# A two-layer hybrid encoder: high and low x as one moving operand for the high gate/up weights, and the filter network moved

## The chip, the cores and the metric

One core of a Trainium2 chip. The metric is the device time of one execution in microseconds, the median of several runs. The profile is one execution of the same program, taken by the hardware profiler.

## The reference

Two layers over x of 256 x 1024, all in float32. A layer is a half-weighted gated feed-forward block, a mixer of three parts, and a second feed-forward block with its own weights.

```python
def swiglu_ffn(x, w_gate, w_up, w_down):
    return (jax.nn.silu(x @ w_gate) * (x @ w_up)) @ w_down

def hyena_filters(L, w1, b1, f1, w2, b2, f2, w3):
...
    h = jnp.sin(f1 * (z @ w1 + b1))
    h = jnp.sin(f2 * (h @ w2 + b2))
    h = (h @ w3).astype(jnp.float32).reshape(L, HY_ORDER, 2, HY_WIDTH)
...
def hybrid_layer(x, ...):
    x = x + 0.5 * swiglu_ffn(rms_norm(x, ffn1_norm), ffn1_w_gate, ffn1_w_up, ffn1_w_down)
    proj = rms_norm(x, mix_norm) @ w_in
...
    x = x + jnp.concatenate([y_hy, y_mla, y_gla], axis=-1) @ w_out
    x = x + 0.5 * swiglu_ffn(rms_norm(x, ffn2_norm), ffn2_w_gate, ffn2_w_up, ffn2_w_down)
    return x
```

The gate and up weights are 1024 x 2816, the down weights 2816 x 1024. The filter network (`hyena_filters`) does not depend on x: z is a constant table of 256 positions by 33, and its hidden width is 64.

## The kernel before

**Split products.** The matmuls run on a rounded float32 form (`F32R`). To keep precision, each operand is split: a high part (the rounded copy) and a low part (what is left of it). A product is three matmuls: high by high, high by low, low by high. `passes` (L1034 to L1038) issues the three: L1036 high weights with high x, L1037 high weights with low x, L1038 low weights with high x. The profile's `xT_high`, `xT_low` are XH and XL, the transposed x of 8 tiles (k) of 128 x 256.

**Weights.** All weights come as a stream of slots of 128 x 2048 (1 MB), fetched by SP into three buffers (`raw`). ScalarE makes the high part of a slot (`hi`, L409), VectorE the low part (`lo`, L681); each has three buffers, too, so that slot n can be converted once slot n - 3 has been used by TensorE. A feed-forward stage has 33 slots: for each of 11 chunks of 256 hidden columns, two gate/up slots (one for each half of 128 hidden columns, gate and up weights of all 8 k) and one down slot.

**A feed-forward stage** (four in all: two in each layer, `f` = 0 and 1). TensorE transposes x (`turn_x`, L1065); ScalarE and VectorE write XH and XL (L425, L691) from the transposes, two tiles a group. Then TensorE runs the two gate/up slots of chunk 0, a row of reciprocal norms (`rstd_row`, L1072), and for every later chunk c: gate/up half 0 of chunk c, half 1 of chunk c, down of chunk c - 1. A gate/up slot (`gate_up`) is 2 x 8 triples of 256 moving columns: for gate (g = 0) and up (g = 1), over the 8 k, accumulated in one half each of a PSUM bank. Banks 4 to 7 hold two chunks' halves (`4 + 2 * pr + half`, where `pr` alternates), banks 0 to 3 the down product. A down slot is 8 triples of 512 columns.

**Each half of a chunk** goes through a chain: VectorE multiplies the gate with the norms' row (`gate_normed`, L706), ScalarE takes the silu (L457), VectorE multiplies with up (`gate`, L710), ScalarE makes the high part of the hidden tile (L461), VectorE the low part (L715). The order on both engines is written out by hand in `ffn` and `chunk`: between `silu` and `ht_high` stands `hi` of the gate/up slot for the next chunk, between `gate` and `ht_low` its `lo`, and after the two halves `hi` and `lo` of a down slot.

**The filter network** runs inside the first stage of each layer (f = 0). GpSimd fetches its tables and weights (`fil`, L361, and the gate weights, L362) once x has been updated (`s_x`), before it computes the reciprocal norms from ScalarE's squares (L334 to L337). TensorE's `filter_mm` (L1144) multiplies by w1 or w2 into bank 7, VectorE's `argument` (L739 to L744) takes bias, frequency and range reduction in eight dependent instructions, ScalarE takes the sine (L465). The first layer of the network stands before chunk 1, the second after the last chunk; `taps_mm` (L1149) with w3 opens the mixer.

**The start.** SP fetches x in two halves of 512 columns, with the first quarter of weight slot 0 between them, then the other quarters of slots 0 and 1, and slot 2. VectorE waits for both x halves and passes their arrival on (`s_x`); TensorE, ScalarE's squares and GpSimd wait for `s_x`.

```python
e.matmul(out, ah, bh, start=start, stop=False)         # passes, L1036
e.matmul(out, ah, bl, start=False, stop=False)         # L1037
return e.matmul(out, al, bh, start=False, stop=stop)   # L1038
```

## Time and profile before

| | |
|---|---|
| median of 3 runs | 1040.7 us (1040.04 to 1040.89) |
| the profiled execution | 1040.12 us |
| its span | 1038.1 us |
| instructions in the span | 17426 |
| mean granted TensorE clock | 0.999 |

The span goes from the first to the last instruction; the execution's own time is 2.0 us longer. "Busy" of an engine is the time in which it has an instruction running. Matmuls overlap: the duration of one is longer than the distance of two starts, so the cost of one in a stream is read from the starts or from a stretch's length over its count. The first layer's stages lie at 5 to 202 us and 331 to 521 us, the mixer between them, and the second layer follows in the same way from 521 us.

### The profile page before, as it was taken

How to read it: one execution, taken by the hardware profiler on the slowest of the kernel's cores; microseconds unless marked ns; L12 is line 12 of the kernel's file. 1: busy time of each engine (PE TensorE's matmuls, PEld its weight loads, DVE VectorE, ACT ScalarE, POOL GpSimd, SP SyncE). 2: the span in 40 equal slices, each digit the busy share in tenths (PEclk: the TensorE clock that was granted, in tenths of full speed). 3: DMA queues.
4: the chain of work that ended last, by engine and by line, in shares of the span. 5: the costliest groups of instructions: out<-in, count | busy, mean ns of one | idle time of the engine just before them, and what ended most of it. 6: DMA issues, size and time to landing. Idle time of an engine off the chain costs nothing.

```text
span 1038.1 us, 17426 instructions
## 1 busy us (share of the span) xinstructions
PE 1010.4 (97%) x7004; PEld 923.8 (89%) x7004; DVE 637.3 (61%) x738; ACT 485.4 (47%) x663; POOL 111.6 (11%) x160
## 2 busy tenths in 40 slices
PE   7999999999899999999999999999998999999997
PEld 6999999888778999999999999997886889999996
DVE  4655555676886655555566555557679765555555
ACT  6544434356654544343354443434566554434342
POOL 2000000150331100000020000003315220000001
PEclk9999999999999999999999999999999999999999
DMA  9565455444303554555555545552542245455551
GB/s 306 188 227 203 167 197 181 143 163 150 135 22 142 202 202 168 197 179 184 183 178 203 203 167 197 179 185 86 199 164 80 81 148 218 167 197 178 186 182 41
DMA packets 27084, 175.93 MB, mean 169 GB/s; under 512 B 3200, under 2 KB 3712, under 8 KB 6560
## 3 DMA queue, kind: packets, MB, share of 16 engines
q1 hardware_dynamic: 25744, 172.90, 46.5%
q0 software_dynamic: 720, 1.95, 0.7%
q8 instruction: 33, 0.54, 0.2%
q10 hardware_dynamic: 576, 0.45, 0.2%
q14 instruction: 11, 0.09, 0.0%
HBM read 174.58 MB, written 1.05 MB: 169 GB/s over the span
## 4 chain that ended last, share of the span: by engine, by line
issue 50%; PE 38%; POOL 9%; DVE 1%; DMA 1%; POOLq 1%; ACT 0%; SPq 0%; DVEq 0%; ACTq 0%
PE psum L1036 13%; PE psum L1037 13%; PE psum L1038 13%; POOL mixer_scratch L350 3%; POOL mixer_scratch L371 1%; POOL mixer_scratch L370 1%; DMA x<-in_x_dram 1%; POOL statistics L323 1%; POOL statistics L321 1%; POOL statistics L334 0%; POOL x_normed L375 0%; DVE x L727 0%; POOL statistics L337 0%; POOLq L226 0%; POOL mixer_scratch L372 0%
## 5 line engine op out<-in xcount | busy, mean ns | idle before, releaser
L681 DVE TENSOR_TENSOR w_low<-w_raw,w_high 128x2048 fp32r<-128x2048 f32 (+1 forms) x160 | 362.8, 2271 | 198.5 <-ACT w_high L409 198.5
L1036 PE MATMUL psum<-xT_high,w_high 128*128 128x256 f32 x1536 | 437.8, 285 | 1.7 <-DVE xT_low L691 1.6
L1037 PE MATMUL psum<-xT_low,w_high 128*128 128x256 f32 x1536 | 435.3, 283 | 0.0
L1038 PE MATMUL psum<-xT_high,w_low 128*128 128x256 f32 x1536 | 435.2, 283 | 0.0
L409 ACT ACTIVATE w_high<-w_raw 128x2048 fp32r<-128x2048 f32 (+1 forms) x160 | 299.1, 1874 | 99.1 <-PE psum L1038 96.3
L1036 PEld LDWEIGHTS psum<-xT_high,w_high 128*128 128x128 f32 x1536 | 295.2, 192 | 5.8 <-issue 4.0
L1037 PEld LDWEIGHTS psum<-xT_low,w_high 128*128 128x128 f32 x1536 | 295.4, 192 | 1.9 <-issue 0.5
L1038 PEld LDWEIGHTS psum<-xT_high,w_low 128*128 128x128 f32 x1536 | 295.4, 192 | 0.0
L457 ACT ACTIVATE silu_gate<-hidden 128x256 f32<-128x256 f32 x88 | 36.8, 418 | 298.9 <-DVE hidden L706 298.9
L1036 PE MATMUL psum<-w_high,hT_high 128*128 128x512 f32 (+1 forms) x360 | 140.0, 389 | 0.0
L1037 PE MATMUL psum<-w_low,hT_high 128*128 128x512 f32 (+1 forms) x360 | 139.7, 388 | 0.0
L1038 PE MATMUL psum<-w_high,hT_low 128*128 128x512 f32 (+1 forms) x360 | 139.2, 387 | 0.0
L1038 PEld LDWEIGHTS psum<-w_high,hT_low 128*128 128x128 f32 x360 | 67.6, 188 | 14.0
L1036 PEld LDWEIGHTS psum<-w_high,hT_high 128*128 128x128 f32 x360 | 67.8, 188 | 13.5 <-issue 0.8
L1037 PEld LDWEIGHTS psum<-w_low,hT_high 128*128 128x128 f32 x360 | 67.8, 188 | 12.3
L706 DVE TENSOR_TENSOR hidden<-psum,diag_rstd 128x256 f32<-128x256 f32 x88 | 37.2, 423 | 67.4 <-PE psum L1038 65.3
L334 POOL TENSOR_TENSOR statistics<-statistics,constants 128x1 f32<-128x1 f32 x14 | 9.1, 647 | 582.8 <-ACT x_normed L419 582.8
L710 DVE SCALAR_TENSOR_TENSOR hidden<-psum,silu_gate 128x256 f32<-128x256 f32 x88 | 37.3, 424 | 42.6 <-ACT silu_gate L457 42.6
L1036 PE MATMUL psum<-w_high,xT_high 128*128 128x512 f32 (+1 forms) x128 | 51.1, 400 | 0.0
L1038 PE MATMUL psum<-w_high,xT_low 128*128 128x512 f32 (+1 forms) x128 | 49.7, 388 | 0.0
L1037 PE MATMUL psum<-w_low,xT_high 128*128 128x512 f32 (+1 forms) x128 | 49.5, 387 | 0.0
L425 ACT ACTIVATE xT_high<-psum,par 128x256 fp32r<-128x256 f32 x64 | 25.1, 486 | 41.9 <-PE psum L1065 25.3
(180 smaller groups left out, 801.9 us busy)
## 6 DMA issues: line engine op xcount, KB each, us to landing
w_raw<-in_w_dram SPq DMA_DIRECT2D x160, 1024.0 KB, 4.8
w_raw<-in_w_dram SPq DMA_DIRECT2D x8, 256.0 KB, 7.9
x<-in_x_dram SPq DMA_DIRECT2D x2, 512.0 KB, 5.8
mixer_scratch<-in_fil_dram POOLq DMA_DIRECT2D x2, 512.0 KB, 6.6
out_dram<-x_normed SPq DMA_DIRECT2D x3, 256.0 KB, 2.1
mixer_scratch<-in_fil_dram POOLq DMA_DIRECT2D x2, 352.0 KB, 6.3
mixer_scratch<-in_fin_dram SPq DMA_DIRECT2D x1, 512.0 KB, 5.5
dft<-in_dft_dram SPq DMA_DIRECT2D x1, 256.0 KB, 5.1
```

The costliest lines, as they stand in the source:

```text
L321: link(l, e.tensor_tensor(b, a, cst[:, inv:inv + n], ALU.mult))
L323: e.tensor_tensor(b, b, cst[:, I_POW:I_POW + n], ALU.pow).then_inc(done.sem, 1)
L350: return e.tensor_tensor(to[:, :, side, :], to[:, :, side, :], o, ALU.add)
L409: e.activation(filled(WH[p], n), filled(raw[p], n), ACT.Copy).then_inc(s_hi.sem, 1)
L425: r = e.activation(by(XH[:, k, :]), halves(PS[:, bank, n * SEQ:(n + 1) * SEQ]), ACT.Copy, scale=par[:, col + k:col + k + 1])
L457: e.activation(sg[:, f, :], hid[:, f, :], ACT.Silu).then_inc(s_silu.sem, 1)
L681: e.tensor_tensor(filled(WL[p], n), filled(raw[p], n), filled(WH[p], n).bitcast(F32), ALU.subtract).then_inc(s_lo.sem, 1)
L706: e.tensor_tensor(hid[:, f, :], PS[:, 4 + 2 * pr + f, 0:SEQ], row, ALU.mult).then_inc(s_gn.sem, 1)
L710: e.scalar_tensor_tensor(out=hid[:, f, :], in0=PS[:, 4 + 2 * pr + f, SEQ:2 * SEQ], scalar=0.5 * float(D) ** 0.5, in1=sg[:, f, :], op0=ALU. ...
L1036: e.matmul(out, ah, bh, start=start, stop=False)
L1037: e.matmul(out, ah, bl, start=False, stop=False)
L1038: return e.matmul(out, al, bh, start=False, stop=stop)
```

## The change

It has four parts.

- XH and XL become one tile, `XB`, with high and low of each k side by side. In a gate/up slot, `split_passes` issues for each k and output tile one matmul of 512 columns (high weights, high and low x) and one of 256 (low weights, high x). Gate and up now have a whole bank each: the left half holds high x high plus low x high, the right half high x low.
- The two halves have to be added. For each half of a chunk ScalarE copies the right halves of both banks into `part` (`part_copy`, 128x512), and VectorE adds the left halves to it into `both` (`add_parts`); norm and gate then read `both` in SBUF. There is one set of banks, no longer two: TensorE waits for the sum (`s_both`) of a half before it starts the same half of the next chunk.
- The filter network moves: `filter_mm` 0 stands between the first two gate/up slots, its argument on VectorE ahead of the low part of slot 2 and its sine on ScalarE ahead of the high part of slot 3; `filter_mm` 1 stands between the gate/up halves of chunk 1, its argument after that chunk's hidden tiles, its sine behind chunk 1. Both use bank 3 and no longer bank 7; the first instruction of the argument has a mark of its own (`f_rd`), for which the first down slot waits. GpSimd fetches the tables once the second pair of high x tiles has been written (`s_xh`).
- At the start both halves of x are fetched before the first weight quarter. TensorE and ScalarE's squares wait for the transfers of x themselves; VectorE waits for none of them.

```diff
-        XH = sb("xT_high", [P, KD, SEQ], F32R)
-        XL = sb("xT_low", [P, KD, SEQ], F32R)
+        XB = sb("xT_split", [P, KD, 2, SEQ], F32R)
+        XH, XL = XB[:, :, 0, :], XB[:, :, 1, :]
...
+        part, both = NV[:, 0], NV[:, 1]
...
             half_x(0, s_in0)
-            part(0, 0)
             half_x(1, s_in1)
-            for n, q in ((0, 1), (0, 2), (0, 3), (1, 0), (1, 1), (1, 2), (1, 3)):
+            for n, q in ((0, 0), (0, 1), (0, 2), (0, 3), (1, 0), (1, 1), (1, 2), (1, 3)):
...
-                e.wait_ge(s_x.sem, s_x.at(l, 4))
+                e.wait_ge(s_xh.sem, s_xh.at(l, 2))
...
+            def part_copy(l, q, f, slot):
+                e.wait_ge(s_used.sem, used(l, slot))
+                e.activation(part, PS[:, 4 + 2 * f:6 + 2 * f, SEQ:2 * SEQ], ACT.Copy).then_inc(s_part.sem, 1)
...
-                hi(l, base + 2); hi(l, base + 3)
+                hi(l, base + 2)
+                part_copy(l, f * CH, 0, base)
+                if f == 0:
+                    sine(l, 0, H1)
+                hi(l, base + 3)
...
                     for h in range(2):
+                        if c is not first:
+                            part_copy(l, q, h, base + 3 * c - 4 + h)
                         silu(l, q, h)
+                        if c is first and h == 0:
+                            part_copy(l, q, 1, base + 1)
...
-                    sine(l, 0, H1)
+                    sine(l, 1, H2)
...
-            def gate_normed(l, q, f, pr, slot):
-                e.wait_ge(s_used.sem, used(l, slot))
-                e.tensor_tensor(hid[:, f, :], PS[:, 4 + 2 * pr + f, 0:SEQ], row, ALU.mult).then_inc(s_gn.sem, 1)
+            def add_parts(l, q, f):
+                e.wait_ge(s_part.sem, s_part.at(l, 2 * q + f + 1))
+                e.tensor_tensor(both, PS[:, 4 + 2 * f:6 + 2 * f, 0:SEQ], part, ALU.add).then_inc(s_both.sem, 1)
+
+            def gate_normed(l, q, f):
+                e.wait_ge(s_both.sem, s_both.at(l, 2 * q + f + 1))
+                e.tensor_tensor(hid[:, f, :], both[:, 0, :], row, ALU.mult).then_inc(s_gn.sem, 1)
...
-                e.scalar_tensor_tensor(out=hid[:, f, :], in0=PS[:, 4 + 2 * pr + f, SEQ:2 * SEQ], scalar=0.5 * float(D) ** 0.5, in1=sg[:, f, :],
+                e.scalar_tensor_tensor(out=hid[:, f, :], in0=both[:, 1, :], scalar=0.5 * float(D) ** 0.5, in1=sg[:, f, :],
...
-                lo(l, base + 2); lo(l, base + 3)
+                if f == 0:
+                    argument(l, 0, 3, C_FB1, C_FF1)
+                lo(l, base + 2)
+                add_parts(l, f * CH, 0)
+                lo(l, base + 3)
...
                     for h in range(2):
-                        gate_normed(l, q, h, 1 - pr, base + h if c is first else base + 3 * c - 4 + h)
+                        if c is not first:
+                            add_parts(l, q, h)
+                        gate_normed(l, q, h)
                         gate(l, q, h, 1 - pr)
                         if c is not first:
                             lo(l, base + 3 * c - 1 + h, pos(base + 2 + h))
+                        elif h == 0:
+                            e.wait_ge(s_h.sem, s_h.at(l, 2 * q + 1))
+                            add_parts(l, q, 1)
                         ht_low(l, q, h, 1 - pr)
+                    if f == 0 and c is first:
+                        argument(l, 1, 3, C_FB2, C_FF2)
                     lo(l, base + 3 * c + 1, pos(base + 1))
...
-                if f == 0:
-                    argument(l, 0, 7, C_FB1, C_FF1)
...
-            e.wait_ge(s_in0.sem, 16)
-            e.sem_inc(s_x.sem, 2)
-            e.wait_ge(s_in1.sem, 16)
-            e.sem_inc(s_x.sem, 2)
-            e.wait_ge(s_cst.sem, 16)
+            e.sem_inc(s_x.sem, 4)
...
+            def split_passes(out, ah, al, k):
+
+                e.matmul(out, ah, XB[:, k, :, :], start=k == 0, stop=False)
+                return e.matmul(out[:, 0:SEQ], al, XH[:, k, :], start=False, stop=k == KD - 1)
...
+                    if f == 0 and first and h == 0 and t * m:
+                        e.wait_ge(f_rd.sem, f_rd.at(l, 2))
...
-                        r = passes(PS[:, 4 + 2 * pr + half, g * SEQ:(g + 1) * SEQ], WH[p][:, k // 2, a], WL[p][:, k // 2, a],
-                                   XH[:, k, :], XL[:, k, :], k == 0, k == KD - 1)
+                        r = split_passes(PS[:, 4 + 2 * half + g, :], WH[p][:, k // 2, a], WL[p][:, k // 2, a], k)
...
                 gate_up(l, turn, base, pos(base), 0, 0, True)
+                if f == 0:
+                    filter_mm(l, 0, F_W1, fil[:, F_Z:F_Z + SEQ], HYE, 3)
                 gate_up(l, turn, base + 1, pos(base + 1), 1, 0, True)
...
                     q = f * CH + (c - 1)
+                    e.wait_ge(s_both.sem, s_both.at(l, 2 * q + 1))
                     gate_up(l, turn, base + 3 * c - 1, pos(base + 2), 0, pr, False)
                     if f == 0 and first:
-                        e.wait_ge(f_arg.sem, f_arg.at(l, 1))
+                        filter_mm(l, 1, F_W2, H1, HYF, 3)
+                    e.wait_ge(s_both.sem, s_both.at(l, 2 * q + 2))
                     gate_up(l, turn, base + 3 * c, pos(base), 1, pr, False)
-
-                    if f == 0 and c is last:
-                        filter_mm(l, 1, F_W2, H1, HYF, 7)
```

## Rows read from the trace of the kernel before

**Rows 1.** The page's busy time of each engine, share of the span, instructions

```profile
PE 1010.4 (97%) x7004; PEld 923.8 (89%) x7004; DVE 637.3 (61%) x738; ACT 485.4 (47%) x663; POOL 111.6 (11%) x160
```

**Rows 2.** The page's costliest groups: operation, shapes, count, busy and mean, idle before

```profile
L1036 PE MATMUL psum<-xT_high,w_high 128*128 128x256 f32 x1536 | 437.8, 285 | 1.7 <-DVE xT_low L691 1.6
```

**Rows 3.** Busy time by stretch: two gate/up slots, one down slot of a steady chunk

```profile
94.06:105.57 11.51, 11.51 (x98) 11.51 (x97) 5.84 (x6) 4.44 (x4) 0.00 (x0) 1.00 0.53 182
105.57:111.05 5.48, 5.48 (x27) 4.52 (x26) 3.42 (x4) 2.53 (x3) 0.00 (x0) 1.00 0.55 191
```

**Rows 4.** The timeline of TensorE, two starts 30 matmuls of 512 columns apart

```profile
193.98 0.39 PE L1036 MATMUL psum<-w_high,hT_high 128*128 128x512 f32 x1
...
200.78 0.39 PE L1036 MATMUL psum<-w_high,hT_high 128*128 128x512 f32 x1
```

**Rows 5.** The timeline of TensorE where a down slot gives way to gate/up

```profile
76.84 0.39 PE L1038 MATMUL psum<-w_high,hT_low 128*128 128x512 f32 x1
77.07 0.28 PE L1036 MATMUL psum<-xT_high,w_high 128*128 128x256 f32 x1
77.18 0.28 PE L1037 MATMUL psum<-xT_low,w_high 128*128 128x256 f32 x1
```

**Rows 6.** The timeline of VectorE and ScalarE in a steady chunk, one half

```profile
100.00 0.42 DVE L706 TENSOR_TENSOR hidden<-psum,diag_rstd 128x256 f32<-128x256 f32 x1 [1.51 <-PE psum L1038]
102.72 2.29 DVE L681 TENSOR_TENSOR w_low<-w_raw,w_high 128x2048 fp32r<-128x2048 f32 x1 [1.38 <-ACT w_high L409]
104.93 0.42 DVE L715 TENSOR_TENSOR hT_low<-hidden,hT_high 128x256 fp32r<-128x256 f32 x1
...
100.79 1.90 ACT L409 ACTIVATE w_high<-w_raw 128x2048 fp32r<-128x2048 f32 x1
```

**Rows 7.** Groups of ScalarE and VectorE by shape: PSUM copy, PSUM add

```profile
L502 ACT ACTIVATE mixer_scratch<-psum 128x512 f32<-128x512 f32 x28 | 16.1, 605 | 19.3 <-PE psum L1199 6.9 <-PE psum L1234 5.1 <-PE psum L1334 4.3
...
L898 DVE TENSOR_TENSOR mixer_scratch<-psum,mixer_scratch 128x512 f32<-128x512 f32 x8 | 5.1, 680 | 0.0
```

**Rows 8.** The timeline of the filter network's matmuls, its argument, and the taps

```profile
535.67 0.64 PE L1144 MATMUL psum<-mixer_scratch 33*64 33x256 f32 x2
536.25 0.38 PE L1036 MATMUL psum<-xT_high,w_high 128*128 128x256 f32 x1
...
26.66 0.53 DVE L739 TENSOR_SCALAR mixer_scratch<-psum,par 64x256 f32<-64x256 f32 x1
...
29.43 0.41 DVE L706 TENSOR_TENSOR hidden<-psum,diag_rstd 128x256 f32<-128x256 f32 x1
...
202.23 1.98 PE L1149 MATMUL psum<-mixer_scratch 64*128 64x512 f32 x4
```

**Rows 9.** The timeline at the start of the second layer's first stage

```profile
522.41 3.23 DVE L691 SCALAR_TENSOR_TENSOR xT_low<-psum,par,xT_high 128x256 fp32r<-128x256 f32 x8 [0.62 <-ACT xT_high L425]
...
522.50 1.71 POOL L361 DMA_DIRECT2D mixer_scratch<-in_fil_dram  x3 [179.46 <-DVE x L727]
...
523.43 0.36 PE L1036 MATMUL psum<-xT_high,w_high 128*128 128x256 f32 x1 [0.50 <-DVE xT_low L691]
```

**Rows 10.** The filter pack's transfers: issue and landing (layer 0, layer 1), GpSimd afterwards

```profile
10.12 1.71 POOL L361 DMA_DIRECT2D mixer_scratch<-in_fil_dram  x3 [7.93 <-DVEq L886]
...
DMA to landing us min/median/max: 7.9/8.0/8.4
...
DMA to landing us min/median/max: 4.4/4.7/4.8
...
15.99 1.68 POOL L334 TENSOR_TENSOR statistics<-statistics,constants 128x1 f32<-128x1 f32 x1 [3.57 <-ACT x_normed L419]
```

**Rows 11.** The start: the timeline, and TensorE's stretch 11.20 to 14.74

```profile
9.58 0.88 DVE L691 SCALAR_TENSOR_TENSOR xT_low<-psum,par,xT_high 128x256 fp32r<-128x256 f32 x2 [7.95 <-DMA x<-in_x_dram]
...
11.20 0.55 PE L1036 MATMUL psum<-xT_high,w_high 128*128 128x256 f32 x1
...
11.20:14.74 3.54, 3.54 (x17) 1.00 1.08 401
```

More of the change, by code:

```diff
@@ L417, in squares @@
                     c = T_SS + 2 * t + n
-                    e.wait_ge(s_x.sem, s_x.at(l, 4 * j + 1 + i))
+                    if l == 0 and j == 0:
+                        e.wait_ge((s_in0, s_in1)[n].sem, 16)
+                    else:
+                        e.wait_ge(s_x.sem, s_x.at(l, 4 * j + 1 + i))
                     e.activation(xn[:, t, n * 512:(n + 1) * 512], x[:, t, n * 512:(n + 1) * 512], ACT.Square,
@@ L780, in ffn @@
                 ht_low(l, q, 0, pr)
-                gate_normed(l, q, 1, pr, base + FFN_SLOTS - 3)
+                add_parts(l, q, 1)
+                gate_normed(l, q, 1)
                 gate(l, q, 1, pr)
@@ L784, in ffn @@
                 if f == 0:
-                    argument(l, 1, 7, C_FB2, C_FF2)
                     lo(l, S_G3)
@@ L1060, in turn_x @@
                 for g in range(4):
-                    e.wait_ge(s_x.sem, s_x.at(l, 4 * j + (2 if g < 2 else 4)))
+                    if l == 0 and j == 0:
+                        e.wait_ge((s_in0 if g < 2 else s_in1).sem, 16)
+                    else:
+                        e.wait_ge(s_x.sem, s_x.at(l, 4 * j + (2 if g < 2 else 4)))
                     for n in range(2):
```

16 lines of the change are left out of this document (9 added, 7 removed).

## The prediction, made before the change was run

> **What bounds the kernel now.** The page's busy times come first: TensorE is busy for 97% of the span, VectorE 61%, ScalarE 47% [rows 1]. So the question is what TensorE spends there, and whether anybody else is close behind. The groups of instructions show the gate/up matmuls of 256 columns to be the largest item, 1536 triples, with almost no idle time before them [rows 2]. 1408 of the triples belong to the four feed-forward stages (22 weight slots of 16 triples, four times).
>
> The stretches show what a matmul costs in its stream: a slot pair of gate and up, 96 matmuls of 256 columns, takes 11.51 us, 119.9 ns each, and a down slot, 24 of 512 columns, takes 5.48 us, 228.3 ns each [rows 3]. The starts of a longer stream of 512 columns stand 226.7 ns apart (30 steps from 193.98 to 200.78) [rows 4]. At 2.4 GHz 256 columns are 106.7 ns and 512 are 213.3 ns. Both shapes thus pay about 13 ns over their columns, per matmul and not per column; where the stream changes shape the same 0.23 and 0.11 to 0.12 us stand [rows 5].
>
> Then the other two engines within a chunk of 17.0 us (two gate/up slots, one down slot) [rows 3, 6]: VectorE norms a gate half (0.42 us), ScalarE takes its silu, makes the next slot's high part (1.9 us), VectorE makes the low part (2.3 us), and so once per slot. TensorE does not wait for any of it. The low part of the slot for the next chunk's first half is done 11 us into the chunk (102.72 + 2.29 = 105.01 against a start at 94.06).
>
> **The main term: one matmul of three goes.** Per k tile and output tile, three matmuls of 256 columns become one of 512 (high weights against high and low x) and one of 256. Columns are the same; one matmul's surplus goes. From the stretches: 3 x 119.9 = 359.7 ns before, 228.3 + 119.9 = 348.2 after, 11.5 ns less; by the long stream's 226.7 it is 13.1 ns less [rows 3, 4]. I take 12.5 ns, nearer to the stream with more steps. 1408 x 12.5 ns = 17.6 us; the ends are 16.2 and 18.4 us.
>
> In cases where TensorE is held by something else in that stretch the term isn't earned. In the first slot of each stage it is paced by VectorE, which writes a low x tile each 0.40 us (eight in 3.23) [rows 9] where the old triple needs 0.36: 8 of 16 pairs gain nothing, 4 x 8 x 12.5 ns = 0.4 us. Sum so far -17.2 us.
>
> The Trainium skill (TensorE: Matmul & The Clock Gate, Wait — 56ns, not 53.3ns?) puts the fixed cost of a matmul in a warm stream at about 2.5 ns. By that section of the Trainium skill the term would be 1408 x 2.5 ns = 3.5 us (rival b); the stretches show 13 ns instead, and the measurement decides.
>
> **The evacuation.** The high and low products now stand in two halves of a bank, so each slot needs a ScalarE copy of 128x512 from PSUM and a VectorE add of 128x512. Nearest rows: 605 ns for such a copy, 680 ns for such an add [rows 7]. With the 0.42 us that they precede, that is 1.3 us more on each half's chain, 2.6 us in a chunk, 1.2 of it on ScalarE and 1.4 on VectorE. Where is it hidden? A chunk has one set of banks less: TensorE now waits for the sum of half 0 before it starts the next chunk's half 0. That bank is finished 5.6 us into the chunk and wanted at 16.6; copy and add need 1.5 us. The same holds for half 1. For weights: the low part that was ready 11 us in is ready some 12.4 us in and is wanted at 16.6. That 4 us is the cover of the steady chunk; I cost it at nothing. If both new operations took double, 2.6 us more, it would still hold.
>
> VectorE and ScalarE as one serial chain: from norming one half to norming the next takes 100.00 to 105.35, some 5.3 us when neither waits for TensorE; plus 0.7 it is 6.0, twice, and 2.2 for the down slot's low part: 14.2 us against TensorE's 16.6 [rows 6, 7]. Behind by something, the pair catches up 2.4 us a chunk.
>
> **The filter network**, in the first stage of each layer. Its two small matmuls cost TensorE as before: from 535.67 to 536.25, 0.6 us, with some 0.1 for the first matmul after [rows 8]. They move: the first between the first two slots, the second between the halves of chunk 1. Its argument is 2.8 us on VectorE (26.66 to 29.43) [rows 8]; before, the first stood ahead of chunk 1 and the second at the stage's end. Nothing is gained at the end: the taps matmul there starts without a wait already [rows 8]. What is late instead is chunk 1 and 2. For layer 1, in the old trace's times [rows 6 to 9]: first slot from 523.43 to 529.2, small matmul to 530.0, second slot and rstd row to 536.1; VectorE's argument to 532.9, low part, sum, low part to 538.0; sum and norm of the two halves to 542.5; second argument (its matmul is at 541.7) to 545.3; low part of the down slot to 547.6. TensorE wants it at 542.4 + 5.56 = 548.0: 0.3 us to spare. Next low part 551.0 to 553.3, wanted at 553.4: 0.1 to spare. The one behind it, 6.0 us later, ends 559.3 and is wanted at 559.0: 0.4 us of stall. From there the chain gains on TensorE. With 0.8 us an add and a copy the stall is 0.8, with 1.0 us an add 1.2. I take 0.4 in each layer, 0.8 us; ends 0 and 2.5. In the second stage of a layer the argument is absent and the down slot's low part has about 2 us to spare: nothing.
>
> The fetch of the filter pack moves behind the second high x group. In layer 1 that is 1.3 us later than 522.50; landing takes at most 4.8 us, so the first piece is there by 528.6, 0.6 us before TensorE asks [rows 9, 10]. In layer 0 it took 7.9 us from 10.12 to 18.0 amid weight transfers [rows 10]; issued at about 11.4 it lands between 18.1 and 19.3, wanted at 18.6. I take nothing, with 0.7 us as the other end. GpSimd's four issues end 1.3 us later too, but after them it sat idle for 3.57 us until ScalarE's squares were there [rows 10], so this costs nothing. The weight slots of SP stay in order; only quarter 0 changes place.
>
> **The start.** Both x halves are issued before weight quarter 0. The second half of x landed at 9.4 and everything of VectorE waited for it (idle 7.95 us) [rows 11]. Now the quarter lands where x did, at about 9.4, as the bytes ahead of it are the same; ScalarE converts it by 10.0, VectorE has its low part at 10.7, and the first gate matmul starts at 10.8 in place of 11.20. From there VectorE sets the pace as before, 1.39 us for two tiles. I take -0.3 us; ends +0.5 (quarter late, ScalarE's queue held behind it) and -0.8. TensorE runs here at the lower level of its clock: 17 matmuls in 3.54 us are 0.21 us for 256 columns, which is 1.2 GHz, though the granted clock of the stretch reads 1.00 [rows 11]. There the surplus is absent and so is the gain (some six triples, 0.1 us, within the ends). If the rise came later, each triple would cost 0.28 us more; 2 us is a bound for the rest of that slot. The Sin and Silu of ScalarE shared one table before (no load ahead of Sin); if a second load of 1.28 us is needed it falls into ScalarE's wait for the argument.
>
> **Sum.** -17.6 + 0.4 + 0.8 - 0.3 = -16.7 us. The profiled execution took 1040.1 us (span 1038.1), so 1023.4 there; the median shown is 0.6 above it: 1024.0 us.
>
> **Rivals.**
> (a) The filter network costs more than it was given: late pack in layer 0, both chains of chunk 1 and 2 late by 1 to 2.5 us each. For it: spare times of 0.1 and 0.3 us on the path. Against: three chunks later all is caught up. Time: 1024.0 + 3.5 = 1027.5. Chance 0.17.
> (b) The surplus goes with x's columns, not with matmuls: a matmul of 512 columns of x costs 2 x 120 = 240 ns. For: no row shows one with gate/up operands. Against: the down stream's 227 ns. The term falls to zero, stalls remain: 1041, and down to 1037 if a fifth of it is fixed. The fixed cost in the Trainium skill (TensorE: Matmul & The Clock Gate, Wait — 56ns, not 53.3ns?) is about that fifth. Chance 0.04.
> (c) Slower: the weight load. A load is shown as 0.19 us and now the next high weights' load lies behind a 256-column matmul of 0.12 us, with a 512-column one ahead. If it starts only when that one has ended, 0.07 us are exposed per pair, 1408 x 0.07 = 99 us, 1125. It decides from 12 ns per pair on. Against: in the old stream every load lies behind 0.12 us and none is exposed [rows 3]. Chance 0.03.
> (d) It goes better: surplus at its upper end, no stalls, start at its best: -18.9 us, 1021.8. Chance 0.1.
> The forecast has the remaining 0.66.
>
> **Numbers.** The range takes in (d), (a) and the forecast's own ends: 1021.5 to 1029.0. A difference under 0.2% (2.1 us) can't be told from none. Faster 0.93, same 0.03, slower 0.04.
>
> **What would show it.** In the profile after: 1408 fewer matmuls; a steady chunk of 16.6 us in place of 17.0; the two gate/up slots at 11.1 us; no wait of TensorE for the sums; a wait of under 1 us for a low part in the third or fourth gate/up slot after the small matmuls; ScalarE copies of 0.6 us and VectorE adds of 0.7 us. A chunk of still 17.0 us makes the main term wrong; waits for the sums in steady chunks make the evacuation wrong; more than 1.5 us per layer around chunks 1 and 2 is rival (a).

## The result and the profile after

The changed kernel takes 1030.3 us (median of 4 runs, 1030.28 to 1030.62) against 1040.6 us for the kernel before beside it: a ratio of 0.9903 (95% interval 0.9888 to 0.9919). It is faster by 10.3 us, where 16.7 us were forecast; the predicted 1024.0 us and the end of the range, 1029.0 us, are both missed. The profiled execution took 1030.28 us, its span is 1028.3 us.

The page of the changed kernel, busy time of each engine and four of its groups (line, operation, shapes, count, busy and mean, idle before):

```profile
PE 1001.0 (97%) x5596; PEld 846.5 (82%) x5596; DVE 694.3 (68%) x826; ACT 537.3 (52%) x752; POOL 110.9 (11%) x160
...
L1070 PE MATMUL psum<-xT_split,w_high 128*128 128x512 f32 x1408 | 501.6, 400 | 4.2 <-DVE w_low L702 2.4
...
L1071 PE MATMUL psum<-xT_split,w_low 128*128 128x256 f32 x1408 | 395.6, 281 | 0.0
...
L462 ACT ACTIVATE mixer_scratch<-psum 128x512 f32<-128x512 f32 x88 | 52.5, 596 | 167.4 <-PE psum L1071 167.4
...
L723 DVE TENSOR_TENSOR mixer_scratch<-psum,mixer_scratch 128x512 f32<-128x512 f32 x88 | 60.4, 687 | 63.5 <-ACT mixer_scratch L462 62.9
```

The 1408 matmuls are gone (7004 to 5596, [rows 1]), the copy costs 0.60 us and the add 0.69 us, near the prices taken from [rows 7], and TensorE has next to no idle time in the gate/up stream. It waits for no sum: of the 4.2 us idle before the long matmuls, 2.4 are put down to low weights, at the start of the kernel, and none to `add_parts`. So the busy times are as forecast, and the time is not. The stretches of a steady chunk, two gate/up slots and one down slot (the columns of [rows 3]):

```profile
94.17:105.46 11.29, 11.29 (x65) 9.80 (x64) 6.94 (x7) 5.05 (x5) 0.00 (x0) 1.00 0.47 186
105.46:110.97 5.51, 5.51 (x27) 4.51 (x26) 3.61 (x6) 3.12 (x4) 0.00 (x0) 1.00 0.49 190
```

The two slots went from 11.51 us [rows 3] to 11.29, not to 11.1: 0.22 us for 32 pairs, where 0.40 were forecast. TensorE is busy throughout, at a granted clock of 1.00. The timeline of TensorE within them (start, duration):

```profile
99.81 0.40 PE L1070 MATMUL psum<-xT_split,w_high 128*128 128x512 f32 x1
100.04 0.28 PE L1071 MATMUL psum<-xT_split,w_low 128*128 128x256 f32 x1
100.16 0.40 PE L1070 MATMUL psum<-xT_split,w_high 128*128 128x512 f32 x1
100.40 0.28 PE L1071 MATMUL psum<-xT_split,w_low 128*128 128x256 f32 x1
100.52 0.40 PE L1070 MATMUL psum<-xT_split,w_high 128*128 128x512 f32 x1
100.76 0.28 PE L1071 MATMUL psum<-xT_split,w_low 128*128 128x256 f32 x1
100.87 0.40 PE L1070 MATMUL psum<-xT_split,w_high 128*128 128x512 f32 x1
```

Three pairs take 1.06 us (99.81 to 100.87): 353.3 ns each, where 360 - 12.5 = 347.5 ns were forecast. The starts do not stand evenly. In nanoseconds, the matmul behind a 512 starts 241, 236 and 233 later, the one behind a 256 starts 120, 113 and 117 later, and so on in a cycle of three pairs (here and below "a 512" is a matmul of 512 moving columns, "a 256" one of 256).

Where the 9.8 us of span went, from TensorE's starts at each stage's border:

| stretch, us | before | after | difference |
|---|---|---|---|
| to the first transpose | 5.22 | 5.58 | +0.36 |
| feed-forward, layer 0, first | 197.01 | 194.88 | -2.13 |
| mixer, layer 0 | 128.61 | 127.84 | -0.77 |
| feed-forward, layer 0, second | 189.99 | 187.81 | -2.18 |
| feed-forward, layer 1, first | 191.61 | 189.41 | -2.20 |
| mixer, layer 1 | 128.59 | 127.87 | -0.72 |
| feed-forward, layer 1, second | 189.77 | 187.58 | -2.19 |

Two things ask for an explanation: each stage gained 2.2 us and not 4, and each mixer gained 0.75 us although the change touches nothing in it. The entry of the first mixer, VectorE's rows in the timeline of the changed kernel:

```profile
194.95 2.29 DVE L698 TENSOR_TENSOR w_low<-w_raw,w_high 128x2048 fp32r<-128x2048 f32 x1 [1.38 <-ACT w_high L411]
197.16 1.44 DVE L748 SCALAR_TENSOR_TENSOR x<-psum,statistics,x 128x512 f32<-128x512 f32 x2
...
199.21 0.75 DVE L748 SCALAR_TENSOR_TENSOR x<-psum,statistics,x 128x512 f32<-128x512 f32 x1 [0.61 <-PE psum L1066]
```

and in that of the kernel before, with ScalarE's two rows ahead of them:

```profile
195.69 0.42 ACT L465 ACTIVATE mixer_scratch<-mixer_scratch 64x256 f32<-64x256 f32 x1 [3.25 <-DVE mixer_scratch L744]
196.02 1.90 ACT L409 ACTIVATE w_high<-w_raw 128x2048 fp32r<-128x2048 f32 x1
197.95 2.29 DVE L681 TENSOR_TENSOR w_low<-w_raw,w_high 128x2048 fp32r<-128x2048 f32 x1 [2.29 <-ACT w_high L409]
200.16 2.06 DVE L727 SCALAR_TENSOR_TENSOR x<-psum,statistics,x 128x512 f32<-128x512 f32 x3
```

Before, ScalarE stood idle for 3.25 us until VectorE's argument was done, took the sine, and only then made the high part of the mixer's first slot; VectorE stood idle for 2.29 us until that was done, made the low part, and ran three updates of x back to back: it was late. The chain is argument, sine, high part, low part, update of x. Now the third update waits 0.61 us for TensorE's down matmul: VectorE has caught up.

### The profile page after: what moved, and what is told of

Its sections match the earlier page's. It is cut to its first block, busy times and chain, and to the rows that moved or that the text cites. A ratio compares the mean times of both kernels' runs of the same rounds, so it can differ in the third digit from the quotient of the medians.

```text
span 1028.3 us, 14899 instructions
## 1 busy us (share of the span) xinstructions
PE 1001.0 (97%) x5596; PEld 846.5 (82%) x5596; DVE 694.3 (68%) x826; ACT 537.3 (52%) x752; POOL 110.9 (11%) x160
## 4 chain that ended last, share of the span: by engine, by line
issue 50%; PE 38%; POOL 9%; DVE 1%; DMA 1%; ACT 1%; POOLq 1%; SPq 0%; ACTq 0%; DVEq 0%
PE psum L1070 16%; PE psum L1071 8%; PE psum L1064 5%; PE psum L1066 4%; PE psum L1065 4%; POOL mixer_scratch L352 3%; POOL mixer_scratch L373 1%; POOL mixer_scratch L372 1%; DMA w_raw<-in_w_dram 1%; POOL statistics L325 1%; POOL statistics L323 1%; POOL x_normed L377 0%; POOL statistics L336 0%; ACT xT_split L430 0%; POOL statistics L339 0%
## 5 line engine op out<-in xcount | busy, mean ns | idle before, releaser
L1070 PE MATMUL psum<-xT_split,w_high 128*128 128x512 f32 x1408 | 501.6, 400 | 4.2 <-DVE w_low L702 2.4
L1071 PE MATMUL psum<-xT_split,w_low 128*128 128x256 f32 x1408 | 395.6, 281 | 0.0
L1070 PEld LDWEIGHTS psum<-xT_split,w_high 128*128 128x128 f32 x1408 | 265.0, 188 | 72.9 <-issue 6.9
L1071 PEld LDWEIGHTS psum<-xT_split,w_low 128*128 128x128 f32 x1408 | 266.6, 189 | 1.4
L462 ACT ACTIVATE mixer_scratch<-psum 128x512 f32<-128x512 f32 x88 | 52.5, 596 | 167.4 <-PE psum L1071 167.4
L723 DVE TENSOR_TENSOR mixer_scratch<-psum,mixer_scratch 128x512 f32<-128x512 f32 x88 | 60.4, 687 | 63.5 <-ACT mixer_scratch L462 62.9
L731 DVE SCALAR_TENSOR_TENSOR hidden<-mixer_scratch,silu_gate 128x256 f32<-128x256 f32 x88 | 37.4, 425 | 42.6 <-ACT silu_gate L466 42.6
L1064 PE MATMUL psum<-w_high,xT_split 128*128 128x512 f32 (+1 forms) x128 | 51.2, 400 | 0.0
L1066 PE MATMUL psum<-w_high,xT_split 128*128 128x512 f32 (+1 forms) x128 | 49.6, 387 | 0.0
L1065 PE MATMUL psum<-w_low,xT_split 128*128 128x512 f32 (+1 forms) x128 | 49.6, 387 | 0.0
L352 POOL TENSOR_TENSOR mixer_scratch<-mixer_scratch 128x128 f32<-128x128 f32 x56 | 33.9, 606 | 98.7 <-ACT silu_gate L550 95.4
## 6 DMA issues: line engine op xcount, KB each, us to landing
w_raw<-in_w_dram SPq DMA_DIRECT2D x160, 1024.0 KB, 4.8
```

The source lines that it names most:

```text
L352: return e.tensor_tensor(to[:, :, side, :], to[:, :, side, :], o, ALU.add)
L462: e.activation(part, PS[:, 4 + 2 * f:6 + 2 * f, SEQ:2 * SEQ], ACT.Copy).then_inc(s_part.sem, 1)
L723: e.tensor_tensor(both, PS[:, 4 + 2 * f:6 + 2 * f, 0:SEQ], part, ALU.add).then_inc(s_both.sem, 1)
L731: e.scalar_tensor_tensor(out=hid[:, f, :], in0=both[:, 1, :], scalar=0.5 * float(D) ** 0.5, in1=sg[:, f, :], op0=ALU.mult, op1=ALU.mult).t ...
L1070: e.matmul(out, ah, XB[:, k, :, :], start=k == 0, stop=False)
L1071: return e.matmul(out[:, 0:SEQ], al, XH[:, k, :], start=False, stop=k == KD - 1)
```

## The experiments

The theories at the outset: a matmul of 512 and one of 256 columns in turn cost more than each does in a stream of its own shape; against it, that something of the kernel (evacuation, banks, reading x side by side) holds TensorE back. The stage lengths and start distances below are worked out from TensorE's starts, as above.

**Bare streams.** A kernel that computes nothing of the reference: matmuls of the same kind on fixed tiles, 48 or more of each sort, behind 120 others. The stream in turn in one bank, as one example:

```diff
+for g in range(2):
+    for k in range(8):
+        e.matmul(PS[:, 3, :], w(W, g, k), X[:, k, :, :], start=k == 0, stop=False)
+        e.matmul(PS[:, 3, 0:256], w(V, g, k), X[:, k, 0, :], start=False, stop=k == 7)
```

> Streams of matmuls alone, nothing else running, each with new weights: 512 columns only, 256 only, 512 and 256 in turn in one bank, the same in two banks, 8 of 512 then 8 of 256, two and two, 128 only, 384 and 384 in turn, 512 and 128 in turn. Theory A (the change of shape costs): 512 only 227 ns, 256 only 120 ns, a pair in turn 353 ns in one bank and in two, a pair of the 8-and-8 stream 347 to 349 ns, two-and-two in between, 384 and 384 as 2 x 173.5. Theory B (a 512-column read of the split x costs more than one of weights): 512 only some 233 to 236 ns already, the 8-and-8 pair 353 ns. Theory C (the 256-column matmul writes the half of the bank just written): one bank 353 ns, two banks 347 ns. Theory D (contention with the transfers and the other engines): every pair here 347 ns.

Measured, from start to start: 512 alone 227.3 ns (226.7 once the first five have passed), 256 alone 119.9 (120.0), so 346.7 to 347.2 for a pair; in turn 353.3, with one bank and with two; eight and eight 349.2; two and two 348.3. So the loss lies in TensorE's own stream: no other engine runs here, and the bank doesn't matter. Two of one width, 384 and 384 in turn, cost 346.7 a pair behind the first. At this point it looked as if each change of width cost some 3 ns.

**Three changed kernels** went with it. Eight matmuls of 512 and then eight of 256 in each output tile:

```diff
-                        r = split_passes(PS[:, 4 + 2 * half + g, :], ...)
+                        e.matmul(out, WH[p][:, k // 2, a], XB[:, k, :, :], start=k == 0, stop=False)
+                    for k in range(KD):
+                        r = e.matmul(out[:, 0:SEQ], WL[p][:, k // 2, a], XH[:, k, :], start=False, stop=k == KD - 1)
```

> The changed kernel with the matmuls of a gate or up tile reordered: 8 of 512 columns, then 8 of 256, in place of one and one. Theory A: 7 of 8 changes of shape are gone, 6 ns for each pair: 1408 x 7/8 x 6.3 ns = 7.8 us faster than the changed kernel, 1022.5 us. Theories B and D: the same time as the changed kernel, 1030.3. Theory C: about as A, as the 256-column matmuls then follow one another in their half (no rival to A here; the streams tell them apart).

1028.3 us (ratio 0.9884, 0.9869 to 0.9898). Three stages are 1.0, 0.7 and 1.0 us shorter than in the changed kernel, but the first is 1.1 us longer. The bare 4.1 ns a pair would be 1.4 us a stage. The traces say where the first stage lost. In its first slots TensorE ran at the lower level of its clock (a 512 each 0.427 us, a 256 each 0.213) up to 20.36 us, where the changed kernel left it at 16.44 and the kernel before at some 15.5. Its waits for low weights there come to 2.8 us, against 2.4. The four runs of this kernel lie within 0.7 us, so the loss isn't one execution's alone; whether the grouping makes the clock rise late was not tested. The price of a pair is better read from the other three stages.

Seven of eight pairs as three matmuls of 256 again, the rest as changed:

```diff
+                if k == 0:
                     e.matmul(out, ah, XB[:, k, :, :], start=True, stop=False)
+                else:
+                    e.matmul(out[:, 0:SEQ], ah, XH[:, k, :], start=False, stop=False)
+                    e.matmul(out[:, SEQ:2 * SEQ], ah, XL[:, k, :], start=False, stop=False)
```

> The changed kernel with three matmuls of 256 columns again in 7 of 8 k tiles, everything else (evacuation, filter network, start) as changed. If the form of the matmuls is all that gained: 1232 x 6.6 ns = 8.1 us slower than the changed kernel, 1038.4, and the 2.2 us left to the kernel before, less the 1.2 us of the k = 0 tiles, are what the other parts gain: 1.0 us. If the other parts cost, as I forecast, 1041 or more.

1036.4 us (0.9963, 0.995 to 0.9976): seven eighths of the pairs (1232) are worth 6.1 us. Against the kernel before, this one is 3.9 us faster, of which the eighth pair can bring 1.2 (176 x 6.7 ns). Evacuation, banks, network and start are those of the change here, and in sum they don't cost but bring the other 2.7 us. By the stages of its trace 1.5 of them lie in the two mixers and 0.9 in the first stage, where its first gate matmul starts at 10.08 us and the clock rises at 14.4; in the changed kernel these are 11.10 and 16.44. That part is of this trace's start.

The second argument, but for its first instruction, and the second sine back at the stage's end:

```diff
-                        argument(l, 1, 3, C_FB2, C_FF2)
+                        argument(l, 1, 3, C_FB2, C_FF2, rest=False)
...
                 if f == 0:
+                    argument(l, 1, 3, C_FB2, C_FF2, first=False)
                     lo(l, S_G3)
```

> The changed kernel with the last seven instructions of the second argument and the second sine back at the end of the stage, where the kernel before had them. Theory: there they delayed the low part of the mixer's first slot and with it the update of x, 0.7 us a layer: 1.4 us slower than the changed kernel, 1031.7. Rival (my forecast, nothing is gained at the end): the same or up to 0.2 us faster.

1035.8 us (0.9957, 0.9944 to 0.997): 5.5 us slower than the change, 2.6 us in each mixer. VectorE's timeline at the first mixer shows how:

```profile
198.43 2.29 DVE L698 TENSOR_TENSOR w_low<-w_raw,w_high 128x2048 fp32r<-128x2048 f32 x1 [2.29 <-ACT w_high L411]
200.64 2.06 DVE L748 SCALAR_TENSOR_TENSOR x<-psum,statistics,x 128x512 f32<-128x512 f32 x3
...
203.72 0.29 DVE L715 TENSOR_SCALAR diag_rstd<-constants,statistics 128x128 f32<-128x128 f32 x1 [1.02 <-POOL statistics L339]
```

The diagonal is made at 203.72 against 200.28 in the changed kernel. It is the chain of the kernel before again (the sine at 196.17, the high part at 196.50), and longer behind TensorE than it was there: the last low part of a hidden tile starts at 193.53, 1.1 us later than in the kernel before, with two sums ahead of it, while TensorE is through with the stage 1.4 us earlier.

**Four more.** Two and two in every gate/up slot; the moved network alone in the kernel before; the quarter of weights fetched between the halves of x again; each copy and add done twice.

```diff
+                    for k2 in range(0, KD, 2):
+                        for k in (k2, k2 + 1):
+                            e.matmul(out, WH[p][:, k // 2, a], XB[:, k, :, :], start=k == 0, stop=False)
+                        for k in (k2, k2 + 1):
+                            r = e.matmul(out[:, 0:SEQ], WL[p][:, k // 2, a], XH[:, k, :], start=False, stop=k == KD - 1)
```

> In every gate/up slot of the changed kernel the two matmuls of 512 of k and k + 1 stand together, then their two of 256. Theory A (a pair costs 353.3 ns in turn and 348.4 ns two and two, as the bare streams showed): 1408 x 4.9 ns = 6.9 us less on the four stages, some 1.7 us each; less in the first slot of a stage, which the low x tiles pace; so 1030.3 - 6.3 = 1024.0 us, and no loss in the first stage, since no matmul is moved past a wait. Theory B (what the grouping by eight lost in the first stage comes from somewhere else than the paced slot, or the pair in the kernel doesn't follow the bare stream): 1027 us or more, with pairs of over 350 ns.

1022.8 us (1022.57 to 1022.95; 0.983, 0.9817 to 0.9844): 7.5 us less than the change, and no stage loses. The gate/up slots of a steady chunk:

```profile
93.72:104.86 11.14, 11.14 (x65) 9.72 (x64) 7.00 (x7) 5.05 (x5) 0.00 (x0) 1.00 0.51 188
```

11.14 us for 32 pairs are 348.1 ns each, as in the bare stream.

The network alone has the change's edits to `argument`, `sine` and `filter_mm`, on the kernel before.

> The kernel before, with the filter network moved as the change moves it (bank 3, mark for its first instruction) and nothing else. Theory A (the second argument and sine at the stage's end held the low part and then the mixer's x update back by some 0.75 us in each mixer, and nothing waits for them in their new place): 2 x 0.75 us less, 1039.1 us, with mixers of 127.9 us in place of 128.6. Theory B (as predicted: nothing is gained at the end, and the new place costs up to 0.4 us in each layer): 1040.6 to 1041.4 us.

1038.2 us (0.9979, 0.997 to 0.9988), its span 1.5 us shorter: -0.71 and -0.73 us in the mixers and nothing, within 0.1, in any stage. This is the gain of the mixers, shown by itself: ScalarE makes the high part at 193.08 there and VectorE the low part at 195.02, each 2.9 us earlier than in the kernel before. Theory B, the step of the prediction, falls.

```diff
             half_x(0, s_in0)
+            part(0, 0)
             half_x(1, s_in1)
```

> The changed kernel with the first weight quarter fetched between the halves of x, as before the change. Theory A (the order is worth little either way: first gate matmul at 11.2 in place of 11.1 us): 1030.3 us, within 0.4. Theory B (the order brought most of what the first stage gained beyond the matmuls): 1031 to 1032 us, all in the first stage.

1031.7 us (1030.92 to 1031.77; 0.9916, 0.9902 to 0.9929), 0.6 us more in the span, all at the start: the transposes of the second half of x, which stand ahead of the first gate matmul, wait until 10.21 us for it, and that matmul starts at 11.83 us in place of 11.10. One start alone can't show 0.6 us: the first gate matmul lies anywhere from 10.08 to 11.33 in the kernels that share the change's start. Counted from the first transpose it comes after 6.37 us here, after 5.98 and 6.13 in the two kernels with the old start (the kernel before, the network alone), and after 5.01 to 5.78 in the nine kernels with the change's order. It is nearer to theory B: the order is worth 0.6 us by the spans of the two profiled executions and 1.4 by the medians; the intervals of the two ratios overlap, so the size isn't shown.

```diff
+                e.activation(KA[...], PS[:, 4 + 2 * f:6 + 2 * f, SEQ:2 * SEQ], ACT.Copy)
                 e.activation(part, PS[:, 4 + 2 * f:6 + 2 * f, SEQ:2 * SEQ], ACT.Copy).then_inc(s_part.sem, 1)
...
+                e.tensor_tensor(KI[...], PS[:, 4 + 2 * f:6 + 2 * f, 0:SEQ], part, ALU.add)
                 e.tensor_tensor(both, PS[:, 4 + 2 * f:6 + 2 * f, 0:SEQ], part, ALU.add).then_inc(s_both.sem, 1)
```

> The changed kernel with each evacuation copy and each add done twice (the first time into a tile that nobody reads): 0.6 us more on ScalarE and 0.7 us more on VectorE for each half of a chunk. Theory A (some 4 us of cover in a steady chunk, as predicted; only chunks 1 and 2 of each stage have little to spare): steady chunks still of 16.8 us, 0 to 0.8 us more in each stage, 1030.3 to 1033.5 us. Theory B (the sums are near the path): each chunk later by 0.5 us or more, over 1050 us.

1040.2 us (0.9998, 0.9989 to 1.0007): 9.9 us more, between the two theories, and the traces say where. A steady chunk is unchanged (two gate/up slots, one down slot):

```profile
97.31:108.60 11.29, 11.29 (x65) 9.79 (x64) 7.26 (x8) 6.47 (x8) 0.00 (x0) 1.00 0.58 214
108.60:114.11 5.51, 5.51 (x27) 4.51 (x26) 4.39 (x6) 2.56 (x4) 0.00 (x0) 1.00 0.39 132
```

The cost is at the edges: 3.4 and 2.8 us in the stages with the network, 1.0 and 0.9 us in the others, 1.2 us at each mixer. There TensorE waits for low parts, as at the first down slot of layer 0:

```profile
37.45 2.28 DVE L699 TENSOR_TENSOR w_low<-w_raw,w_high 128x2048 fp32r<-128x2048 f32 x1
...
39.78 0.50 PE L1066 MATMUL psum<-w_high,hT_high 128*128 128x512 f32 x1 [0.55 <-DVE w_low L699]
```

So the cover of the steady chunk is real, and the thin places are the ones named in the prediction: the first chunks behind the network, where 0.1 to 0.3 us were to spare.

**What makes a pair cost 353 ns.** "Each change of width costs 3 ns" fits the numbers badly: two and two has half the changes but saves four fifths. Hence more bare streams.

```diff
+hi(4, r % 2, k); lo(4, r % 2, k, t=W)        # one weight tile for both
+hi(5, r % 2, k); lo(5, r % 2, k, m=7 - k)    # another k of x for the short one
+hi(6, r % 2, k, 448); lo(6, r % 2, k, 320)
```

> Bare streams again (nothing of the reference is computed), each at least 48 pairs of one matmul of 512 and one of 256 columns or near it. A pair costs 347.2 ns with no change of width and 353.3 ns in turn. Theory A (each change of width costs some 3 ns, whichever way): the turned order (512, 256, 256, 512) and two and two 350.3 ns, four and four 348.7 ns; 512, 256, 256 in turn 473.3 ns; 448/320 and 400/368 in turn 353.3 ns like 512/256. Theory B (the cost comes with the short one: the weight load for the next matmul has only the short one's time to hide in): it is less for 448/320 and nothing for 400/368 (347 ns), more for 512/192 (over 30 ns above 26.5 + 704/2.4), and two and two costs less than A says since every second load lies under a long one. Theory C (it is the other weights' or x's place in memory): one weight tile for both, or another k of x for the short one, brings 347 ns; A and B expect 353.3 there.

In the order they ran, in ns a pair: turned order 348.7, two and two 348.2, four and four 350.5, one weight tile 346.8, another k 346.7, then 448/320 and 400/368 both 353.3, and 512, 256, 256 at 467.3 (226.7 + 2 x 120.0 = 466.7); 512 and 192 in turn, last, 344.5. Theory A is out (equal numbers of changes of width cost 346.7 and 353.3, and the three cost what they do alone), B too (400/368, for which it expected 347, costs 353.3). C seemed right, twice.

> Bare streams a third time (nothing of the reference is computed), 48 pairs of 512 and 256 columns each, in this order, told apart by their place in time: 1 in turn, plain; 2 the short one a tile behind (512 of k + 1, then 256 of k); 3 one weight tile for both; 4 plain again; 5 low weights of 7 - k; 6 the two weight tiles exchanged; 7 the short one reads low x of k; 8 it reads high x of k + 1; 9 low weights of k - 1; 10 it reads a copy of x in another tile; 11 it reads high x of k - 1; 12 its weights come from a third tile 256 bytes off. Theory C (the 6 ns come where weights or x are read at certain places in memory): 1 and 4 again 353.3 ns, 3 again 347; of the others those that take the conflict away 347 and the rest 353. Theory D (the stream falls into one of two rhythms by chance, whatever it reads): 1 and 4 differ, or 3 is 353. Theory A (width alone) is out if 3 is 347 again.

Eleven cost 353.3 ns and the second 352.5, the one weight tile included, which had been 346.8 in the run before. C is out and D stands: the same instructions on the same tiles run at one of two prices. What differed was the execution and what had run ahead of them: four and four there, a stream in turn here. The next bare run separates the two.

The kernel with the short matmul a tile behind went with it:

```diff
+                    for k in range(KD + 1):
+                        if k < KD:
+                            e.matmul(out, WH[p][:, k // 2, a], XB[:, k, :, :], start=k == 0, stop=False)
+                        if k:
+                            r = e.matmul(out[:, 0:SEQ], WL[...], XH[:, k - 1, :], start=False, stop=k == KD)
```

> The changed kernel with the short matmul of each pair a tile behind (512 of k + 1, then 256 of k), so that two neighbours read different tiles of x. Theory C: a pair of 347 ns as in the bare stream where the short one read another k, 1408 x 6.6 ns = 9.3 us less than the changed kernel, less some 0.5 us in the paced slots: 1021.5 us. Theory A (the cost goes with the changes of width, of which there are as many): 1030.3 us. Theory D: anywhere between.

1028.4 us (0.9886, 0.9869 to 0.9902): theory C expected 1021.5. Within its slots the slow cycle of three pairs stands, interrupted once in an output tile where two 512 meet. A steady chunk gains 0.07 us: 0.03 in its two gate/up slots (11.26 us against 11.29), and 0.05 in its down slot, whose matmuls settle at 227 ns behind the first two.

```diff
+                for n in lead:
...
+                        groups(b, 0, n)
+                for r in range(3):
+                    q = groups(b, r % 2, 1)
```

> Bare streams (nothing of the reference is computed): twelve times 24 matmuls of 512 columns, then a lead, then 24 pairs of 512 and 256 in turn. The leads, each of one or more runs over 8 k: none; 4+4; twice 4+4; three times 4+4; 2+2; three times 2+2; 8+8; a single 256; four 256; 8+8 then 2+2; 2+2 then 8+8; a single 384. Theory D (a stream in turn keeps one of two rhythms, 346.7 or 353.3 ns a pair, and what stands ahead of it decides which): with no lead 353.3 ns as in the kernel's slots, and at least one lead after which all 24 pairs cost 346.7 ns. Theory E (the fast rhythm of one earlier run belongs to that execution, not to its lead): 353.3 ns after all twelve.

Each lead has its rhythm, and the 24 pairs keep it to the end, all within one execution: theory E is out. No lead, 8+8, one or four 256, a single 384, 8+8 then 2+2, and 2+2 then 8+8: 353.3 ns over their second halves. 4+4 (once, twice, three times) and 2+2 (once, three times): 346.7. The fast price comes in two patterns, an even one behind 4+4 (230 and 117 ns) and a cycle of two pairs behind 2+2 (233, 118, 230, 112 ns). And the last eight pairs alone do not decide: 2+2 brings the fast price behind a stream of 512, and the slow one behind 8+8. The timeline, with no lead, first 512 and the 512 twenty pairs on:

```profile
34.45 0.39 PE L58 MATMUL psum<-xT_split,w_high 128*128 128x512 f32 x1
...
41.50 0.40 PE L58 MATMUL psum<-xT_split,w_high 128*128 128x512 f32 x1
```

and behind 4+4:

```profile
51.15 0.40 PE L58 MATMUL psum<-xT_split,w_high 128*128 128x512 f32 x1
...
58.09 0.39 PE L58 MATMUL psum<-xT_split,w_high 128*128 128x512 f32 x1
```

7.05 and 6.94 us for the same 40 matmuls.

**Is it so in the kernel?** Only eight of a chunk's 32 pairs are regrouped, as a lead:

```diff
+                    step = 2 if g == 0 and half == int(first) else 1      # 4 in the second kernel
+                    for k0 in range(0, KD, step):
+                        for k in range(k0, k0 + step):
+                            e.matmul(out, WH[p][:, k // 2, a], XB[:, k, :, :], start=k == 0, stop=False)
+                        for k in range(k0, k0 + step):
+                            r = e.matmul(out[:, 0:SEQ], WL[p][:, k // 2, a], XH[:, k, :], start=False, stop=k == KD - 1)
```

> The changed kernel; only the eight gate pairs of the first gate/up slot after a down slot (and of the second slot of a stage) stand two and two, all others in turn as in the change. Theory D (those eight set the rhythm of the 24 pairs in turn behind them): 347 ns for each of the 24, 348.5 for the eight, so over a chunk 24 x 6.6 + 8 x 4.8 = 197 ns less than the changed kernel, x 40 chunks = 7.9 us, and some 0.3 in the first chunks: 1022.2 us, a little less than with all pairs two and two (1022.8). Theory A (each change of width costs 3 ns): only the eight gain, 40 x 8 x 4.9 ns = 1.6 us: 1028.7 us.

1022.1 us (1021.55 to 1022.55; 0.9826, 0.9813 to 0.984). The windows of a steady chunk:

```profile
93.24:104.33 11.09, 11.09 (x65) 9.70 (x64) 6.98 (x7) 5.05 (x5) 0.00 (x0) 1.00 0.52 189
104.33:109.78 5.45, 5.45 (x26) 4.51 (x25) 3.55 (x6) 3.13 (x4) 0.00 (x0) 1.00 0.55 192
```

Within them stand 24 pairs in turn exactly as in the change, now at 347 ns, in the cycle of two pairs (233, 117, 231, 112 ns):

```profile
99.83 0.39 PE L1174 MATMUL psum<-xT_split,w_high 128*128 128x512 f32 x1
...
100.52 0.39 PE L1174 MATMUL psum<-xT_split,w_high 128*128 128x512 f32 x1
...
101.22 0.39 PE L1174 MATMUL psum<-xT_split,w_high 128*128 128x512 f32 x1
```

Eight regrouped pairs alone would have brought 1.6 us; 8.2 us came. The down slot gains too, 5.45 us against 5.51: its first 512 start 233, 231 and then 226 to 227 ns apart, in place of 224 to 241 for the first ten. This trace's first stage gains 0.6 us more than the others; there TensorE was at the higher level of its clock from its first gate matmul on. The median stands 0.5 us above this execution.

> The same with the eight leading pairs four and four. Theory D: as in e13_lead_two but 350 ns for the eight: 40 x (24 x 6.6 + 8 x 3.3) ns = 7.4 us less, 1022.8 us. Theory A: 1028.5 us. If the rhythm isn't kept from one slot to the next: 40 x 16 x 2.5 ns more.

1023.5 us (1023.19 to 1023.94; 0.9838, 0.9825 to 0.9852), 6.8 us less than the change, with the even pattern (230 and 117 ns) in its 24 pairs. The rhythm as the cause of the shortfall holds in the kernel. The lead of two is the fastest version found; from two and two throughout (1022.8 us) it differs by less than the intervals tell apart.

## Why the prediction was wrong, and where it was right

**The main term failed, in its size.** The step was "from the stretches: 3 x 119.9 = 359.7 ns before, 228.3 + 119.9 = 348.2 after", taken at 12.5 ns for each of 1408 pairs. The change brings 360 - 353.3 = 6.7 ns, 9.4 us in place of 17.6. The step added prices of two pure streams for a mixed one. That sum is just what the fast rhythm costs (226.7 + 120.0 = 346.7 ns); the change as it was built runs in the slow one, of which no row before it could tell. The evidence offered for it, "where the stream changes shape the same 0.23 and 0.11 to 0.12 us stand" [rows 5], was two starts read to a hundredth of a microsecond, in which 6 ns can't be seen. A clue was there: [rows 3] and [rows 4] disagreed by 1.6 ns a matmul, and I took a value between them. They disagree because the first five matmuls of a down slot, behind the stream of 256, start 228 to 236 ns apart. A mixed stream was the question, and the one place of the trace that mixed shapes was averaged away. The gain itself exists: in the other rhythm a pair is 346.7 ns, 13 ns less than the triple, and the kernel with a lead of two gets it. Why one lead brings one rhythm and another the other stays open.

**"Nothing is gained at the end" failed, with its sign.** It rested on the taps matmul starting without a wait [rows 8]. But the argument held back ScalarE's sine, the sine the high part behind it, and these the low part, VectorE's update of x and the diagonal: 0.75 us a mixer, 1.5 us in all, shown by the network alone. The wait looked at belonged to the wrong instruction.

**The filter network's stalls, 0.8 us, came as some 0.2**, and rival (a) did not come. The chain was right as it was worked out: in layer 1 its third low part, the one forecast to be 0.3 us late, is done at 554.46 us and its slot starts at 554.54; in layer 0 the same one is done at 49.32 and TensorE starts at 49.38, 0.07 us behind its pace, and loses 0.1 more at that restart. The chunk that came out 0.2 us longer than forecast gave some of that room, and not all: with a lead of two the chunk takes 16.5 us, as forecast, and the same slot is again only 0.06 us late (549.80 to 549.86). That the spare time was thin is seen from the doubled sums: 0.6 us more a copy and 0.7 us more an add, and the stages with the network lose 3.4 and 2.8 us.

**The evacuation at nothing was right** in the steady chunk, even at double cost, as said. "It would still hold" was said of the steady chunk only; for the whole kernel it does not.

**The start**: -0.3 us forecast. The first gate matmul came 0.10 us earlier, at 11.10, the first transposes 0.36 us later; within the ends. The later rise of the clock that the prediction priced is there too: the granted clock is 0.50 from 13.03 to 16.44 us, behind a wait of TensorE of 1.87 us, and the old kernel's matmuls were at their fast distance from 15.5 us on. The second table load of ScalarE came in layer 0 (at 21.41 and 26.93 us) and fell into its waits.

**The rivals**: (b), a surplus that goes with the columns of x, is out, since matmuls of high weights over 512 columns of x start 226.7 ns apart in a stream of their own. The Trainium skill's 2.5 ns for the fixed cost (TensorE: Matmul & The Clock Gate, Wait — 56ns, not 53.3ns?) would make the gain 3.5 us, an estimate from that section; a merged triple saves 6.7 or 13.3 ns here, by rhythm, and the measurement decides. (c), an exposed weight load of 0.07 us a pair, is out. Whether a piece of a load is in the 6.7 ns of the slow rhythm no run tells. For shorter matmuls more stands over the columns: 128 columns alone cost 111.2 ns each (at 2.4 GHz their columns take 53.3), and 512 and 128 in turn 340.0 ns for 266.7 ns of columns, 73 over, where 512 and 256 are 27 to 33 over. Whether that is the load isn't shown. Two slips of the prediction change nothing here: 99 us on its forecast are 1123 and not 1125, and "same 0.03, slower 0.04" should stand the other way round, as (b) had 0.04 and (c) 0.03.

By terms, against the forecast in brackets: pairs -9.4 (-17.6), first slots and what else is in the stages +0.7 (+0.4), network some 0.2, counted within that (+0.8), and mixers -1.5 (0), start +0.4 (-0.3): -9.8 (-16.7) us of span. The start of +0.4 is the first transpose; what it gives back up to the first gate matmul lies in the stages.

## What to carry to other kernels

The price of a mixed stream need not be the sum of the prices in pure ones: look for the mixture in the trace, read it over tens of instructions and not over two starts, and where it isn't there, give the term a range from nothing up. Where matmuls of two widths alternate, try another order of a few of them, and measure it in the kernel itself, as the same order acts differently behind another stream; here it brought 8.2 us on top of the change's 10.3 and cost no instruction. When work is moved away from a border, ask of every engine there which instruction is late, not only of the one with the most work, and follow what stands behind it in program order on the next engine.

## What the runs showed of the hardware

- A stream of 512 and 256 columns in turn has two stable prices: 346.7 ns a pair, either even (230 and 117 ns) or in a cycle of two pairs (233, 118, 230, 112), and 353.3 ns a pair in a cycle of three (236, 113, 233, 117, 241, 120). Which one it takes depends on what has run ahead of it, not on the last eight pairs alone, and it keeps it over 48 pairs at least. Why was not settled: no run separates weight loading from the fetch of the moving data here.
- The price doesn't depend on the PSUM bank (seen at 353.3), on the weight tile or on the tile of x, in streams that are otherwise alike. 448/320 and 400/368 in turn were only seen at 353.3, 384/384 only at 346.7.
- Behind a stream of 256, the first five matmuls of 512 start 228 to 236 ns apart (233, 236, 228, 233, 230 in the kernel before) before they settle at 226.7.
- With the first quarter of weights (0.25 MB) fetched between the halves of x (0.5 MB each), TensorE's first gate matmul comes 6.0 to 6.4 us after its first transpose (three kernels); with both halves ahead of the weights it comes after 5.0 to 5.8 us (nine kernels).
